# Levels of a gated recurrence as 64 by 64 products in alternating column halves, and the forget gates' bounds computed earlier

## The reference

```python
lb = jax.nn.softmax(lower_bounds, axis=0)
lb = jnp.cumsum(lb, axis=0) - lb[0]              # bounds of the forget gates, from parameters alone
k = (1.0 - lb) * jax.nn.sigmoid(-z)              # for each direction
log_f = jnp.logaddexp(jnp.log(jnp.maximum(lb, LB_FLOOR)), jnp.log1p(-lb) + jax.nn.log_sigmoid(z))
...
# per head, over keys s <= t (and, flipped, s >= t):
decay = jnp.exp(g[t] - g[s])                     # g: running sum of log_f, for each of 128 channels
attn[t, s] = sum_d q[t, d] * k[s, d] * decay[t, s, d]
o = attn @ v + (q * exp(g)) @ state
```

## Time and profile before

| | us |
|---|---|
| median of 3 runs | 1789.99 (1789.46 to 1790.95) |
| the profiled execution, its own time | 1789.95 |
| its span, first to last instruction | 1788.2 |
| TensorE busy | 1749.2 |
| VectorE busy | 1157.7 |
| ScalarE busy | 858.0 |
| mean granted clock of TensorE | 0.996 |

### The profile page before, as it was taken

One profiled execution on the slowest core, in us unless ns is written; L12 is line 12 of the kernel. 1 busy time (PEld: TensorE's weight loads), 2 busy tenths in 40 slices (PEclk: granted clock), 3 DMA queues, 4 the chain that ended last, 5 costly groups with the idle time before them and its releaser, 6 DMA issues.

```text
span 1788.2 us, 21242 instructions
## 1 busy us (share of the span) xinstructions
PE 1749.2 (98%) x8310; PEld 1440.9 (81%) x8310; DVE 1157.7 (65%) x1699; ACT 858.0 (48%) x1190; POOL 27.0 (2%) x51
## 2 busy tenths in 40 slices
PE   7999999999999999999999899999999999999997
PEld 5788888877878888888888687788888888888886
DVE  6744246778786645677675345767768778768564
ACT  5223234776768413322222223576576567565422
POOL 0000000000000000000000000100000000000000
PEclk9999999999999999999999999999999999999999
DMA  4323222333222222222223223622222222222322
GB/s 158 119 95 121 93 95 91 111 105 95 101 95 88 84 100 95 96 98 95 95 96 104 80 97 117 235 84 83 71 82 72 71 79 75 82 72 78 123 94 83
DMA packets 48419, 174.69 MB, mean 98 GB/s; under 512 B 5552, under 2 KB 5680, under 8 KB 47680
## 3 DMA queue, kind: packets, MB, share of 16 engines
q1 hardware_dynamic: 43712, 155.45, 25.7%
q0 software_dynamic: 4608, 17.89, 3.1%
HBM read 164.87 MB, written 4.26 MB: 95 GB/s over the span
## 4 chain that ended last, share of the span: by engine, by line
PE 92%; DVE 5%; ACT 2%; issue 1%; DMA 0%; SPq 0%; DVEq 0%; ACTq 0%
PE bank L502 80%; PE bank L697 3%; PE bank L520 2%; PE bank L626 1%; PE bank L628 1%; DVE w_low L1327 1%; PE bank L544 1%; PE bank L706 1%; ACT w_high L806 1%; PE bank L588 1%; DVE scaled L1368 0%; PE bank L742 0%; PE bank L731 0%; PE bank L719 0%; DVE Y L1558 0%
## 5 line engine op out<-in xcount | busy, mean ns | idle before, releaser
L502 PE MATMUL bank<-u_high,w_high 128*128 128x512 f32 x1568 | 622.4, 397 | 5.3 <-DVE w_low L1327 5.3
L502 PE MATMUL bank<-u_high,w_low 128*128 128x512 f32 x1568 | 611.0, 390 | 0.0
L502 PE MATMUL bank<-u_low,w_high 128*128 128x512 f32 x1568 | 611.0, 390 | 0.0
L806 ACT ACTIVATE w_high<-raw 128x1024 fp32r<-128x1024 f32 x285 | 300.4, 1055 | 520.9 <-PE bank L502 510.8
L1327 DVE TENSOR_TENSOR w_low<-raw,w_high 128x1024 fp32r<-128x1024 f32 x285 | 348.0, 1222 | 274.1 <-ACT w_high L806 268.6
L502 PEld LDWEIGHTS bank<-u_high,w_high 128*128 128x128 f32 x1568 | 294.6, 188 | 67.8 <-issue 9.6
L502 PEld LDWEIGHTS bank<-u_high,w_low 128*128 128x128 f32 x1568 | 294.4, 188 | 62.5
L502 PEld LDWEIGHTS bank<-u_low,w_high 128*128 128x128 f32 x1568 | 294.7, 188 | 59.4 <-issue 1.7
L502 PE MATMUL bank<-f_high,w_high 128*128 128x512 f32 x176 | 70.6, 401 | 6.7 <-DVE w_low L1327 6.7
L1137 ACT ACTIVATE XL<-XL 128x512 f32<-128x512 f32 x56 | 35.3, 630 | 75.4 <-DVE XL L1780 45.8
L502 PE MATMUL bank<-f_low,w_high 128*128 128x512 f32 x176 | 70.4, 400 | 0.0
(11 more groups left out here) (341 smaller groups left out, 2547.3 us busy)
## 6 DMA issues: line engine op xcount, KB each, us to landing
raw<-stream SPq DMA_DIRECT2D x285, 512.0 KB, 3.2
rows<-running POOLq DMA_DIRECT2D x32, 256.0 KB, 3.7
X<-x_t SPq DMA_DIRECT2D x4, 512.0 KB, 8.0
u_high<-n_high_rows POOLq DMA_DIRECT2D x2, 1024.0 KB, 6.5
u_low<-n_low_rows POOLq DMA_DIRECT2D x2, 1024.0 KB, 9.1
residual<-X POOLq DMA_DIRECT2D x4, 512.0 KB, 7.1
X<-residual POOLq DMA_DIRECT2D x4, 512.0 KB, 5.9
out_t<-X SPq DMA_DIRECT2D x8, 256.0 KB, 2.1
```

Of the source, the lines that this page charges most:

```text
L502: ins = pe.matmul(acc[:], w[:, k], x[:, at + k], start=start and k == first and j == 0, stop=stop and k == KT - 1 and j == 2)
L806: act.activation(w_high[:, n % HI_RING], raw[:, n % RAW_RING], ACT.Copy).then_inc(hi_done, 1)
```

## The change

Each product of a level (128 keys by 128 queries of a chunk) is made as two products, one for each half of the array's columns. Half 0 has the first 64 keys as weights and writes partitions 0 to 63, half 1 the other 64 keys and partitions 64 to 127. Each multiplies 64 queries: those of the same half of the chunk, and in level 1, whose pairs cross the middle, those of the other half. The quarters that no level needs are not written any more. So a level has 8 products, 16 instructions, where it had 4 products, 8 instructions. And `bounds()` moves in both lists from the loop over `down` to the loop over `a_out`, to row 1 of VectorE and row 2 of ScalarE; ScalarE loads the table of Exp and Ln before the `a_out` loop.

```diff
                 wait_for(pe, x_put, at - 1)
+                half = P // 2
                 for c in range(NCH):
-                    cs = slice(c * P, (c + 1) * P)
-                    ins = pe.matmul(side[at % 2][:, cs], XL[:, at % 3, 0, cs], XL[:, at % 3, 1, cs], start=True, stop=True)
+                    for e in range(2):
+                        keys = slice(c * P + half * e, c * P + half * e + half)
+                        other = e if n != 1 else 1 - e
+                        to = slice(c * P + half * other, c * P + half * other + half)
+                        ins = pe.matmul(side[at % 2][half * e:half * e + half, to], XL[:, at % 3, 0, keys],
+                                        XL[:, at % 3, 1, to], start=True, stop=True)
                 ins.then_inc(x_mm, 1)
...
@@ ScalarE @@
+            def bounds():
+
+                act.wait_ge(lb_v, 1)
+                act.activation(lbc[:, 1], lbc[:, 1], ACT.Exp).then_inc(lb_a, 1)
+                act.wait_ge(lb_v, 2)
+                act.activation(lbc[:, 1], lbc[:, 1], ACT.Ln).then_inc(lb_a, 1)
+                act.activation(lbc[:, 2], lbc[:, 2], ACT.Ln).then_inc(lb_a, 1)
+
+            act.preload_act_table_set(LOG_SET)
             for j in range(KT):
                 ahead(("a_out", j))
-
-            table = [""]
+                if j == 2:
+                    bounds()
+
+            table = [LOG_SET]
...
                 if j == 0:
                     act.preload_act_table_set(LOG_SET)
                 else:
-                    if j == 2:
-                        bounds()
                     cast(SECOND_EARLY, j - 1, u_high)
...
@@ VectorE @@
+            def bounds():
+
+                lbr = par[:, PCOL["lower_bounds_2"]:PCOL["lower_bounds_2"] + 2 * KT]
+                tt(lbc[:, 1], lbr, lbr, ALU.subtract).then_inc(lb_v, 1)
+                dve.wait_ge(lb_a, 1)
+                link(dve.reciprocal(lbc[:, 2], lbc[:, 1]))
...
+                ts(lbc[:, 2], lbc[:, 0], LB_FLOOR, 2.0 ** 40, ALU.max, ALU.mult).then_inc(lb_v, 1)
+                dve.wait_ge(lb_a, 3)
+                link(ts(lbc[:, 2], lbc[:, 2], -40.0 * float(np.log(2.0)), None, ALU.add))
+                link(tt(lbc[:, 3], lbc[:, 2], lbc[:, 1], ALU.subtract))
+                link(tt(lbc[:, 4], lbc[:, 1], lbc[:, 2], ALU.subtract))
+
             for j in range(KT):
                 key = ("a_out", j)
                 ahead(key)
+                if j == 1:
+                    bounds()
                 wait_block(dve, key)
...
             for j in range(KT):
                 for part in range(3):
                     ahead(("down", j, part))
-                if j == 1:
-                    bounds()
                 residual(2, j, ("down", j, 2), X, both=True, rows=SECOND_EARLY, weight=w_both[:, j:j + 1])
```

More of the change, by code:

```diff
@@ L1045, in _ @@
                 act.activation(h1_conv[:], h1_conv[:], ACT.Silu).then_inc(f_silu, 1)
[L1046 to L1052, removed]
             for j in range(KT):
@@ L1469, in _ @@
             cp(decay_b[:].rearrange("p c h -> p (c h)"), side[1][:, 0:NCH * HEADS]).then_inc(d_tok, 1)
+            def bounds():
[3 more added lines that the diff above has]
+                link(dve.reciprocal(lbc[:, 2], lbc[:, 1]))
+                link(tt(lbc[:, 1], lbc[:, 1], lbc[:, 2], ALU.mult))
+                link(tt(lbc[:, 0], lbc[:, 1], lbc[:, 1], ALU.subtract))
+                link(ts(lbc[:, 5], lbc[:, 0], -1.0, 1.0, ALU.mult, ALU.add))
+                link(cp(lbc[:, 1], lbc[:, 5]))
+                ts(lbc[:, 2], lbc[:, 0], LB_FLOOR, 2.0 ** 40, ALU.max, ALU.mult).then_inc(lb_v, 1)
[3 more added lines that the diff above has]
+                link(tt(lbc[:, 4], lbc[:, 1], lbc[:, 2], ALU.subtract))
             for j in range(KT):
@@ L1668, in _ @@
                 dve.wait_ge(f_split, j + 1)
[L1670 to L1685, removed]
             for j in range(KT):
```

## The result

The changed kernel takes 1777.07 us (median of 4 runs, 1776.01 to 1777.66), the kernel before 1789.72 beside it: a ratio of 0.9928, 95% interval 0.991 to 0.9945. Forecast were 1776 and a range of 1771 to 1786. The profiled execution took 1776.96 us, its span is 1775.2.

What follows compares the result with a forecast made beforehand. TensorE, busy for 98% of the span, was taken to bound the kernel. 1789.95 less 9.4 us (stop at the down products and its slow clock) and 4.7 us (56 levels) gave 1775.9, say 1776 us; range 1771 to 1786.

Steps and rivals of the forecast that it cites:

- The stop at the down products: Around 1000 us: moving the bounds removes TensorE's wait for `w_low` and the slow clock behind it, 9.4 us.
- The bounds beside the output product: In `a_out`, near 215 us: the moved bounds cost nothing, with 5.6 us of cover before block 4.
- The level: Line 697: a level takes 0.82 us instead of 0.904; over 56 levels a gain of 4.7 us.
- the heads' rows: Lines 626 and 628, source of the costs of entering (0.14 us) and leaving (0.20 us) the column-half form.
- the pitch: Step between instructions in one column half of a level, taken as 0.060 us, between 0.056 and 0.0645.
- the upper bound: Level's slow end: pitch 0.0645 from line 570, second half one pitch late: 0.91 us, a loss of 0.5 us.
- One at a time: Rival: a level's sixteen instructions don't overlap, level 1.24 to 1.37 us, kernel 1799 to 1807 us; chance 0.13.
- half an overlap: Rival: halves catch up only within a product, level 1.06 us, kernel 1789 us, no change; chance 0.08.
- A price per instruction at line 570's pitch: Levels: about 62 ns per matmul from the sequencer's firmware, a level about 1.33 us; no chance of its own.

Runs made afterwards that it cites:

- e1: The changed kernel with the levels' products as they were, so only the bounds are moved: 1781.94 us, ratio 0.9955.
- e5: The new levels, but the bounds left in the `down` loop with ScalarE's part at row 1, VectorE's row, instead of 2: 1776.67 us, ratio 0.9925.
- e6: The changed kernel with ScalarE's part of the bounds at row 4 of the `a_out` loop instead of row 2: 1783.53 us, one run.
- e4: The changed kernel without the products of half 1, 8 instructions a level, half of the scores missing: 1776.74 us, one run.
- e8: The changed kernel with levels 0 and 2 to 6 as 32 by 32 products in column quarters, 32 instructions each: 1764.92 us, one run.
- e3: The changed kernel with all four products of half 0 first, then all four of half 1: 1791.18 us, one run.
- e2: The kernel before with the levels' products in column halves and nothing else changed: 1785.44 us, ratio 0.9973.
- f2: The changed kernel, with two heads' products of the state-space scan also joined by turns of two instructions: 1771.09 us, ratio 0.9892.
- f3: The changed kernel with both the column quarters and the scan's heads by turns: 1760.07 us, ratio 0.9829.
- e7: The changed kernel with each half's products moving all 128 queries of the chunk instead of 64: 1800.40 us, one run.
- f1: The changed kernel with levels 0 and 2 to 6 in column quarters, timed in rounds: 1765.98 us, ratio 0.9862.
- f4: The changed kernel with turns of four instructions (two products of each half) instead of two: 1780.55 us, one run.

## Why the prediction was right

**The stop at the down products.** 9.4 us forecast. e1's trace shows the mechanism gone, e5 and e6 show its cause (the offset of positions in the two lists) and its price per row. With the clock's loss near 1117 us set apart (1.6 us), e1's 8.1 us by the medians are 9.7; by the traces, from the wait near 520 us to the one near 1110 us, 9.3 us fewer pass. The step held in cause, size and place.

**The bounds beside the output product.** Costed at nothing; it is nothing. VectorE had block 4's `w_low` 5.8 us ahead (5.6 were forecast), and e6 shows that two rows more would have used it up.

**The level.** 0.82 us forecast, 0.81 measured: entering 0.14 and leaving 0.21 came over from the heads' rows (0.14 and 0.20), and the pitch is 0.058, between the chosen 0.060 and the half of a full weight load, 0.056. The term was 4.7 us and is 5.1 by the traces. It is a little low because levels in front of transposes gain more (0.14 us; the leaving is cheaper there). Summed over the second block's 72 stretches of small products, each counted like a level, they got 5.6 us shorter, from 107.4 to 101.8; some 0.5 us went into the blocks, whose pitch rose from 0.2280 to 0.2283 us over about 1700 matmuls. The rise lies in the first eight matmuls behind a stretch; why it is there is open. Two numbers of the upper bound were off without moving the forecast: line 570's transposes start 0.062 us apart in the trace, not 0.0645, and 0.40 + 8 x 0.0645 is 0.92, a loss of 0.7 us, not 0.5.

**The rivals.** One at a time, and half an overlap, are refuted for this order by e4 and by the paired loads. A price per instruction at line 570's pitch doesn't hold for them either: e8's 32 pass in 0.39 us. e3 shows what the order decides: with the loops the other way round the change would have gained nothing, at 1791.2 us. The rule of the Trainium skill by which weight loads overlap running matmuls only across row groups (TensorE: Matmul & The Clock Gate, Part 3) doesn't hold here: all of these share their rows. Its statement, in the same part, that matmuls start in program order doesn't hold either: in order, e3's 16 instructions would be 16 steps, and its level is as long as 12.9. That a change of tiling mode drains the engine is in the Trainium skill too (TensorEngine Tiling, Key Properties), and the trace agrees with it, at 0.35 us for there and back.

**What was missing.** The sum had no term for the clock behind the other stops. Near 1112 us (1106 to 1121 in the several kernels) all versions have a stop of 2.8 us, where the second block's rows are made. Behind it the clock stays full in the kernel before, in e2 and e6, f2 and f3; it falls to half for 3.4 us in the changed kernel, in e1, e3, e4, e5, e7, e8, f1 and f4. From that stop's end to the matmul that ends the next stop, 52.2 us pass in the first group and 53.8 in the changed kernel: 1.6 us. In the kernel before:

```profile
1122.00:1126.00 4.00, 2.08 (x9) 1.76 (x10) 3.75 (x5) 3.97 (x5) 2.12 (x4) 1.00 0.87 324
```

So, with the start left out (0.2 us shorter in the changed kernel), the full account of the profiled executions is 1789.95 - 9.4 - 5.1 + 1.6 = 1777.05, against 1776.96 measured. Two small misses, the level's 0.4 and the clock's 1.6, are of opposite signs; the larger alone would have stayed within the range, so it is not their cancelling that made the forecast right. What settles whether the clock falls behind this stop isn't shown. The stop begins at 1109.7 to 1112.1 us in the kernels where the clock falls and at 1106.3, 1107.2, 1119.8, 1121.1 and 1121.1 us in those where it stays, but no run changed the moment alone. Nor is it the kernel alone that decides: `e8` and `f1` are one kernel, and near 57 us the clock falls in the profiled execution of `e8` and not in that of `f1`. Since a trace shows one execution, the 1.6 us are known for the traced ones only.

## What to carry to other kernels

Where a product's result is used in parts only, narrow products in different column groups can leave the rest out; in the shapes tried here each group costs as if alone, provided that the groups take turns of two instructions and that a stretch repays some 0.34 us for entering and leaving. When two engines hand values to each other in hand-written lists, put both ends at the same position: a row between them cost a standstill of VectorE of 14.19 us where a row was three blocks and 4.39 us where it was one, and TensorE stopped only for what its finished blocks didn't cover. A faster stretch of the bounding engine is worth only as much as the others' work beside it allows; here 4.6 us of 18.4.

## What the runs showed of the hardware

- Column groups run side by side, weight loads and matmuls alike, with all rows shared: starts 6 to 8 ns apart, two groups at 0.058 us a step (64 columns, 64 moving; `after`), four at 0.032 (32 and 32; `e8`).
- A later group passes waiting instructions of an earlier one, but over a few only: turns of two cost nothing, of four one step (0.05 us), of eight 4.9 steps (0.28 us).
- The moving part, not the number of instructions, sets the step where it is the longer: 64 columns of weights with 128 moving go at 0.109 us, alone or in two groups.
- A stop of 7 us of TensorE (before) costs 2.5 us more in slow clock behind it, one of 6 us (e6) 2.6; one of 2.8 us costs 1.6 or nothing.
